# Two stick-breaking heads scored together on halves of TensorE's rows, and an earlier split of the first key weights

## The chip, the cores and the metric

The kernel runs on one core of one Trainium2 chip. The time is the device time of one execution in microseconds (us). Times before and after are medians of several executions of the same inputs; the profile is of one more execution.

## The reference, cut to what matters

Two transformer blocks over 512 positions of width 1024 are computed, one after the other. Only the first block matters here. Its input x is normed, scaled and shifted by a modulation that is itself computed from c (`mod = c @ w_ada + b_ada`), and projected by one wide matrix:

```python
h = rmsnorm(x, norm_gain) * (1.0 + scale) + shift
proj = h @ w_in
(sb_q, sb_k, sb_v, sb_z, c_q, c_kv, k_rot, mla_z, g_a, g_b) = split(proj)
# stick-breaking attention, 8 heads of 64, for each block of 128 queries
z = einsum('bhqd,bhkd->bhqk', qb, k) * scale
log_one_minus = where(strict, log_sigmoid(-z), 0.0)
suffix = cumsum(log_one_minus, reverse=True) - log_one_minus
w = where(strict, exp(log_sigmoid(z) + suffix), 0.0)
out = einsum('bhqk,bhkd->bhqd', w, v)
```

The second block has, among other things, a forgetting attention ("fox", also 8 heads of 64) and a per-layer embedding (PLE) whose small projection `p @ w_ple_proj` needs nothing of x; the kernel computes that projection first of all. Inputs and outputs are float32.

## The kernel before, in words

**Engines.** Each engine runs one written-out program (`tensor_program`, `scalar_program`, `vector_program`, `pool_program`, `sync_program`) in its own order. They meet at semaphores. A name such as `SBQK` or `HI` is a semaphore with the count that each key stands for. An engine never passes over a wait: what stands behind it stands still.

**Split weights and activations.** A projection is computed from a high part (float32 rounded to the fp32r format) and a low part (the rest) of weights and activations. One output tile of 128 x 512 with contraction 1024 is 8 x 3 = 24 matmuls of 128 x 512 (`project`, line 673; every matmul is recorded at line 650 in `mm`). The names are `whi`, `wlo` for the weights, `hhi`, `hlo` for the activations h, and `phi`, `plo` for the PLE inputs.

**Weights in chunks.** `chunks()` (line 34) lists the weights in the order of use. A chunk of 128 x 1024 is loaded by SyncE into one of 3 buffers `raw`; ScalarE copies its high part to one of 4 buffers `whi` (line 1341); VectorE subtracts, which gives `wlo` (line 1824). Both engines do that in `conv(name, idx)`, which splits all chunks up to two behind the named one in the list (`LOOK = 2`). A buffer of the four can be written again once the projection of four chunks earlier is done. In the list, the eight chunks that follow the stick-breaking values (cq 0 to 2, ckv 0 and 1, kr, sz 0 and 1) each have a chunk `ada` of the modulation behind them, which VectorE multiplies and sums directly from `raw` (line 1835, into `mod`). In that part of the list, two chunks ahead are one `ada` and one weight chunk only; behind it, two chunks ahead are two weight chunks.

**The first stage.** TensorE does the PLE projection (chunks `pp`), then the stick-breaking queries (`sbq`, four chunks) block by block of h as the modulation comes (`project_group`). ScalarE evicts each block of the turned x twice (`modulated`, line 1380): to `tmpf` in full float32 and to `hhi` rounded; VectorE subtracts for `hlo`. After it TensorE projects `sbk` 0 to 3 and the values `sbv`.

**The stick-breaking stage.** `sb_qk(h)` computes the scores of one head (keys x queries, 512 + 384 + 256 + 128 columns) in three banks of PSUM, with contraction over 128 rows. Two heads share a tile of keys `kp`, so the queries `qp` of each head have a tile of their own of which the other head's 64 rows are zero (written by GpSimd at line 579). Then, for head h: VectorE takes the minimum with 40 (`sb_pre`, line 1988), ScalarE does exp and log(1 + x) (lines 1465 and 1467), VectorE takes a maximum (`sb_pre2`), ScalarE writes the high part `sph`, GpSimd (896 of the columns, line 567) and VectorE (256) write the low part `spl`; TensorE adds the suffix sums (`sb_suffix`), ScalarE does exp (`sb_weights`, line 1480), and `sb_pv` multiplies two heads by the values. `sph` and `spl` are one buffer each, so head h + 1 may write them only after the suffix of head h.

**The fillers.** Between these steps TensorE does 21 further steps of projections, the fillers (`filler_a`, one `yield` for each): cq 0 to 2, ckv 0 and 1, kr, sz 0 to 3, mz 0 to 3, ga 0 to 5, and ga 6 and 7 together. All but one of the first 20 write to bank 7. ScalarE and VectorE run the same generator in their own programs: VectorE copies the filler's bank out and calls `conv` for the coming chunks, ScalarE calls `conv`. Of the fillers named here by number, F0 is cq 0, F5 is kr, F6 is sz 0, F13 is mz 3, F14 is ga 0, F19 is ga 5. The order on TensorE before, for each pair of heads, is: scores of h + 1, filler, suffix of h, filler, scores of h + 2, filler, suffix of h + 1, filler, values of the pair, filler.

The fox stage of the second block has the form that the change brings to the first: `fox_qk` (line 1021) computes the scores of two heads in turn, each with contraction over 64 rows, and then the masks of both.

Of the kernel before, what the change touches and what calls it, by code (L numbers as in the profile page):

```python
# [169 lines left out]
def build(nc, w_all, cst_d, rc_d, gc_d, rm_d, vec_d, x_d, xn_d, c_d, pos_d, ada_d, p_d, out_d):  # L170
# [7 lines left out]
    WN = {i: w for w, i in enumerate(WCH)}  # L178

# [6 lines left out]
    with top:  # L186
# [54 lines left out]
        with ExitStack() as s1:  # L241
            qp = sb(s1, "qp", [128, 8, S])
            kp = sb(s1, "kp", [128, 4, S])
            sbv = sb(s1, "sbv", [128, 4, S])
            sp = sb(s1, "sp", [128, 2, 1280])
            sph = sb(s1, "sph", [128, 1280], F32R)
            spl = sb(s1, "spl", [128, 1280], F32R)
# [116 lines left out]
        def weights_of(name, idx):  # L364
            i = PIDX[name, idx]
            _, _, kb, n = PLAN[i]
            w = WN[i]
            hi, lo = (x[:, w % NHL, 0:kb * n].rearrange("p (k n) -> p k n", k=kb) for x in (whi, wlo))
            return hi, lo, w

# [18 lines left out]
        def turn_bank(h, kb):  # L389
# [45 lines left out]
        QZERO = sig("pool_qzero", (0, 1))  # L435
        QPE, KPE, SBV = sig("act_qp", range(8)), sig("dve_kp", range(4)), sig("act_sbv", range(4))
        SBQK, SBMIN, SBLN, SBMAX, SBHI, SBLO0, SBLO1, SBSUF = (
            sig(n, range(8)) for n in ("pe_sbqk", "dve_sbmin", "act_sbln", "dve_sbmax", "act_sbhi", "pool_sblo",
                                       "dve_sblo", "pe_sbsuf"))
# [109 lines left out]
        def pool_program(e):  # L549
# [10 lines left out]
            def sb_low(h):  # L560
                G.wait_ge(*QZERO(1))
                G.wait_ge(*SBHI(h))
                if h > 1:
                    G.wait_ge(*ROPED("kr"))
                if h:
                    G.wait_ge(*SBSUF(h - 1))
                e.tensor_tensor(spl[:, 0:896], sp[:, h % 2, 0:896], fr(sph[:, 0:896]), ALU.subtract).then_inc(SBLO0.sem, 1)  # L567

# [5 lines left out]

            G.wait_ge(*proj("pp", 1, 3))
            for r in range(2):
                if r:
                    G.wait_ge(*QZERO(0))
                e.memset(qp[64 - 64 * r:128 - 64 * r, :, :].rearrange("p (m r) n -> p m r n", r=2)[:, :, r, :], 0.0
                         ).then_inc(QZERO.sem, 1)  # L580

# [24 lines left out]
            for h in range(8):  # L606
                sb_low(h)
                if h == 1:
                    rope_sum("kr", krs[64:96, :], 0)
# [35 lines left out]
        def tensor_program(e):  # L645
# [32 lines left out]
            def project_group(chs, act, order=range(8), split=True, between=None):  # L678
# [4 lines left out]
                def high(name, idx, m, b, k):  # L683
                    hi, lo, w = weights_of(name, idx)
                    if split:
                        T.wait_ge(*HI(key(k)))
# [83 lines left out]
            for m in range(4):  # L770
                free[m] = [QPE(2 * m + 1)]
# [7 lines left out]
            def filler_a():  # L779
                for m in range(5):  # L780
                    project(*(("cq", m) if m < 3 else ("ckv", m - 3)), 128, 7, h1)
                    free[7] = [CQ(m)]
# [9 lines left out]
                T.wait_ge(*SS(("c", 4)))  # L792
                sum_squares(6, "kv", ssq[:, :])
                for m in range(8):
                    project(*(("sz", m) if m < 4 else ("mz", m - 4)), 128, 7, h1)
                    free[7] = [ZE(m)]
                    yield
                for m in range(6):
                    b = 0 if m == 4 else 7
# [8 lines left out]
            def sb_qk(h):  # L808
                T.wait_ge(*QPE(h))
                T.wait_ge(*QZERO(h % 2))  # L810
                T.wait_ge(*KPE(h // 2))
                T.wait_ge(*CONST())
                for kb in KB_ORDER:
                    out = sb_out(h, kb)
                    bank(3 * (h % 2) + BK[kb])
                    mm(out, kp[:, h // 2, 128 * kb:128 * kb + 128], qp[:, h, 128 * kb:512], kb != 3, False)
                    t = mm(out[:, 0:128], identB, msB, False, False)
                t.then_inc(SBQK.sem, 1)

            def sb_suffix(h):  # L820
# [5 lines left out]
                T.wait_ge(*SBLO0(h))  # L826
                T.wait_ge(*SBLO1(h))
# [23 lines left out]
            sb_qk(0)  # L851
            next(fa)
            for pr in range(4):
                h = 2 * pr
                sb_qk(h + 1)
                next(fa)
                sb_suffix(h)
                next(fa)
                if pr < 3:
                    sb_qk(h + 2)  # L860
# [4 lines left out]
                if pr < 3:  # L865
                    next(fa)
# [469 lines left out]
        def scalar_program(e):  # L1336
# [6 lines left out]
            def conv(name, idx=0, look=LOOK):  # L1343

                while split_to[0] < min(PIDX[name, idx] + 1 + look, len(PLAN)):
# [6 lines left out]
                    if w >= NHL:  # L1352
                        A.wait_ge(*used(w - NHL))
                    copy(whi[:, w % NHL, 0:n], raw[:, i % NRAW, 0:n]).then_inc(WHI.sem, 1)
# [19 lines left out]
            def modulated(b):  # L1374
# [4 lines left out]
                for out in (tmpf[:, b % 2, :], hhi[:, b, :]):  # L1379
                    t = e.activation(out, PB[4 + b % 4][:, :], ACT.Identity, scale=mod[:, 8 + b:9 + b], bias=mod[:, b:b + 1])  # L1380
                t.then_inc(HI.sem, 1)
# [22 lines left out]
            for b in range(NB):  # L1404
                modulated(b)
                if b == 0:
                    conv("sbq", 3, 0)

            conv("sbq", 3)
            for m in range(4):  # L1410
                A.wait_ge(*proj("sbq", m))
                for r in range(2):
                    copy(qp[64 * r:64 * r + 64, 2 * m + r, :], PB[m][64 * r:64 * r + 64, :], scale=0.125
                         ).then_inc(QPE.sem, 1)
# [17 lines left out]
            def filler_a():  # L1432
# [14 lines left out]
                A.wait_ge(*CQN(2))  # L1447
                root(rsb[:, :], 6, 256, "kv")
                for m in range(8):
                    conv(*(("sz", m) if m < 4 else ("mz", m - 4)))  # L1450
# [1192 lines left out]
```

## Time and profile before

| what | value |
|---|---|
| median of 3 executions | 1234.1 us (1234.05 to 1234.74) |
| profiled execution, its time | 1235.34 us |
| its span | 1233.5 us |
| TensorE busy | 97% of the span |
[...]
| chain of work that ended last, share of TensorE | 85% |

The span is from the first to the last instruction in the profile; the execution's own time is 1.8 us longer. A record of a matmul shows its start and a modelled end, and following matmuls overlap, so the time that one takes is read from start to start. "Idle before" in brackets is counted from the modelled end of the record before, which is later than the start at which the next could have followed.

### The profile page before, as it was taken

How to read it: one execution, taken by the hardware profiler on the slowest of the kernel's cores; microseconds unless marked ns; L12 is line 12 of the kernel's file. 1: busy time of each engine (PE TensorE's matmuls, PEld its weight loads, DVE VectorE, ACT ScalarE, POOL GpSimd, SP SyncE). 2: the span in 40 equal slices, each digit the busy share in tenths (PEclk: the TensorE clock that was granted, in tenths of full speed). 3: DMA queues.
4: the chain of work that ended last, by engine and by line, in shares of the span. 5: the costliest groups of instructions: out<-in, count | busy, mean ns of one | idle time of the engine just before them, and what ended most of it. 6: DMA issues, size and time to landing. Idle time of an engine off the chain costs nothing.

```text
span 1233.5 us, 15994 instructions
## 1 busy us (share of the span) xinstructions
PE 1199.7 (97%) x6548; PEld 964.2 (78%) x6548; DVE 701.2 (57%) x1086; ACT 500.9 (41%) x799; POOL 92.3 (7%) x72
## 2 busy tenths in 40 slices
PE   7999999999999999999999999999999999999996
PEld 5787777777777787887777788878888888888885
DVE  6644564359556676457887785364444444433356
ACT  5424434454454455224446545253233223322244
POOL 0390010104000000000000200000000000000000
PEclk9999999999999999999999999999999999999998
DMA  9732322213121343331112101123322222433322
GB/s 370 282 109 71 125 92 84 69 59 101 52 69 52 97 142 98 105 120 45 59 54 84 34 4 36 52 86 103 103 89 100 99 89 98 144 99 100 104 86 71
DMA packets 35593, 118.22 MB, mean 96 GB/s; under 512 B 3936, under 2 KB 6112, under 8 KB 35520
## 3 DMA queue, kind: packets, MB, share of 16 engines
q1 hardware_dynamic: 33024, 111.03, 26.9%
q0 software_dynamic: 1392, 4.72, 1.3%
q10 hardware_dynamic: 1104, 1.45, 0.3%
q8 instruction: 52, 0.85, 0.3%
q14 instruction: 21, 0.17, 0.0%
HBM read 112.99 MB, written 4.19 MB: 95 GB/s over the span
## 4 chain that ended last, share of the span: by engine, by line
PE 85%; DVE 6%; ACT 5%; issue 2%; POOL 0%; DVEq 0%; ACTq 0%
PE pb L650 82%; PE pb L906 1%; DVE wlo L1824 1%; PE pb L736 1%; ACT mP L1539 1%; DVE mnm L2066 1%; DVE xT L1824 1%; ACT whi L1341 1%; ACT Y L1341 1%; DVE mP L2056 1%; DVE junk L1835 0%; PE pb L1068 0%; ACT xT L1560 0%; DVE sp L1824 0%; ACT fv L1341 0%
## 5 line engine op out<-in xcount | busy, mean ns | idle before, releaser
L650 PE MATMUL pb<-hlo,whi 128*128 128x512 f32 (+2 forms) x1056 | 408.9, 394 | 7.1 <-DVE wlo L1824 5.9
L650 PE MATMUL pb<-hhi,wlo 128*128 128x512 f32 (+2 forms) x1056 | 410.8, 389 | 2.6 <-DVE wlo L1824 2.6
L650 PE MATMUL pb<-hhi,whi 128*128 128x512 f32 (+2 forms) x1056 | 409.9, 388 | 0.0
L1824 DVE TENSOR_TENSOR wlo<-raw,whi 128x1024 fp32r<-128x1024 f32 (+1 forms) x178 | 216.1, 1219 | 109.0 <-ACT whi L1341 108.0
L650 PEld LDWEIGHTS pb<-hlo,whi 128*128 128x128 f32 (+1 forms) x1056 | 198.5, 188 | 55.2 <-DVE wlo L1824 8.6
L650 PEld LDWEIGHTS pb<-hhi,wlo 128*128 128x128 f32 (+1 forms) x1056 | 198.1, 188 | 44.0 <-DVE wlo L1824 3.5
L650 PEld LDWEIGHTS pb<-hhi,whi 128*128 128x128 f32 (+1 forms) x1056 | 198.1, 188 | 41.0
L1341 ACT ACTIVATE whi<-raw 128x1024 fp32r<-128x1024 f32 (+1 forms) x178 | 181.5, 1034 | 72.9 <-PE pb L650 67.9
L650 PE MATMUL pb<-alo,whi 128*128 128x512 f32 x176 | 68.5, 389 | 0.0
L650 PE MATMUL pb<-ahi,wlo 128*128 128x512 f32 x176 | 68.5, 389 | 0.0
L650 PE MATMUL pb<-ahi,whi 128*128 128x512 f32 x176 | 68.5, 389 | 0.0
L1341 ACT ACTIVATE ahi<-tmpf 128x512 fp32r<-128x512 f32 x22 | 13.9, 632 | 100.5 <-DVE tmpf L1824 100.5
L1341 ACT ACTIVATE hhi<-xT,vec 128x512 fp32r<-128x512 f32 x16 | 11.6, 724 | 84.4 <-DVE xT L1824 84.4
L1824 DVE TENSOR_TENSOR xT<-xT,pb 128x512 f32<-128x512 f32 x16 | 10.9, 684 | 57.1 <-PE pb L650 57.1
L1824 DVE TENSOR_TENSOR tmpf<-pb,rsb 128x512 f32<-128x512 f32 (+1 forms) x31 | 20.9, 674 | 35.8 <-PE pb L650 29.5
L1762 ACT ACTIVATE tmpf<-tmpf 128x512 f32<-128x512 f32 x22 | 13.9, 632 | 64.3 <-DVE tmpf L1824 64.3
L650 PEld LDWEIGHTS pb<-alo,whi 128*128 128x128 f32 x176 | 33.0, 188 | 6.9
L650 PEld LDWEIGHTS pb<-ahi,wlo 128*128 128x128 f32 x176 | 33.0, 188 | 6.9
L650 PEld LDWEIGHTS pb<-ahi,whi 128*128 128x128 f32 x176 | 33.0, 188 | 6.8
L1824 DVE TENSOR_TENSOR sq<-pb,rsb 128x512 f32<-128x512 f32 x22 | 15.2, 692 | 39.4 <-PE pb L650 39.4
L1539 ACT ACTIVATE mP<-pb,mnm 128x512 f32<-128x512 f32 (+3 forms) x32 | 16.4, 526 | 33.4 <-DVE mnm L2046 33.4
L567 POOL TENSOR_TENSOR spl<-sp,sph 128x896 fp32r<-128x896 f32 x8 | 18.8, 2347 | 127.4 <-ACT sph L1341 127.4
(363 smaller groups left out, 1632.6 us busy)
## 6 DMA issues: line engine op xcount, KB each, us to landing
raw<-w_all SPq DMA_DIRECT2D x173, 512.0 KB, 3.5
adab<-ada_d SPq DMA_DIRECT2D x12, 512.0 KB, 12.5
raw<-w_all SPq DMA_DIRECT2D x10, 384.0 KB, 3.0
xT<-xn_d SPq DMA_DIRECT2D x4, 512.0 KB, 12.9
gbt<-ada_d SPq DMA_DIRECT2D x4, 512.0 KB, 15.7
ple_scratch<-zs SPq DMA_DIRECT2D x8, 256.0 KB, 12.2
xT<-x_d POOLq DMA_DIRECT2D x8, 256.0 KB, 3.2
out_d<-xT SPq DMA_DIRECT2D x6, 256.0 KB, 2.6
```

What stands on the lines that cost most here:

```text
L567: e.tensor_tensor(spl[:, 0:896], sp[:, h % 2, 0:896], fr(sph[:, 0:896]), ALU.subtract).then_inc(SBLO0.sem, 1)
L650: return e.matmul(out, lhs, rhs, start=start, stop=stop, skip_group_check=True)
L736: t = e.matmul(PB[b][:, :], ones, src, start=True, stop=more is None)
L906: t = e.transpose(PB[b][:, o + 128 * (qi - kb):o + 128 * (qi - kb) + 128], P[:, PO[qi] + 128 * kb:PO[qi] + 128 * kb + 128], ident)
L1341: return e.activation(out, in_, ACT.Copy, **kw)
L1539: t = e.activation(d, src, ACT.Exp, bias=nm[:, i, qi:qi + 1], accum_out=rs[:, i, qi:qi + 1])
L1762: e.activation(tmpf[:, j % 2, :], tmpf[:, j % 2, :], ACT.Silu).then_inc(SG.sem, 1)
L1824: return e.tensor_tensor(out, a, b, op)
L2056: t = e.tensor_scalar(d, d, rs[:, i, qi:qi + 1], None, ALU.mult)
L2066: t = e.tensor_reduce(mnm[:, h % 2, qi:qi + 1], src, AX.X, ALU.max)
```

## The change

**Scores on halves of the rows.** `qp` becomes four tiles, one for each pair of heads, without zeros; ScalarE copies each projected tile in one instruction instead of two, and GpSimd's two fills of zeros go. `sb_qk(pr)` computes both heads of a pair, head r with contraction over the 64 rows from 64 r, alternating between the heads, then all the masks. It needs all six banks 0 to 5 at once.

**A new order of the stage.** For each pair: scores of both heads, three fillers in a row, suffix of h, a filler, suffix of h + 1, a filler, values. Fillers with number 1, 6, 11 and 16 write to bank 6. The sum of squares for ckv moves from ahead of sz 0 to ahead of sz 2. ScalarE's order is: exp and log of h, exp and log of h + 1, high part of h, (in the last pair the Silu of sz, with its two table loads), three fillers, high part of h + 1, exp of h, filler, exp of h + 1, filler. VectorE's order is: minimum of h, minimum of h + 1, maximum of h, filler, maximum of h + 1, low part of h, two fillers, low part of h + 1, two fillers. The low part is VectorE's alone; GpSimd does none of it.

**The first keys' weights.** The chunk sbk 0 is split into `phi` and `plo`, which are free once the PLE projection is done. ScalarE does it between the blocks 6 and 7 of h, VectorE ahead of the low part of block 7. The chunks behind it move up one buffer in the ring of four. `qp` moves behind `kp` and `sbv` in memory.

**The modulated blocks.** ScalarE writes `hhi` first, with a semaphore of its own (`HI1`) for which TensorE waits, and `tmpf` second.

```diff
+        def split_at(w, n):
+            if w == WK0:
+                return phi[:, :, :].rearrange("p a b -> p (a b)"), plo[:, :, :].rearrange("p a b -> p (a b)")
+            r = (w if w < WK0 else w - 1) % NHL
+            return whi[:, r, 0:n], wlo[:, r, 0:n]
+        def filler_bank(i):
+            return 6 if i % 5 == 1 else 7
+        def room(w):
+            if w == WK0:
+                return [proj("pp", 1, 3)]
+            at = w - NHL if w < WK0 or w - NHL > WK0 else w - NHL - 1
+            return [used(at)] if at >= 0 else []
...
+            def sb_qk(pr):
+                T.wait_ge(*QPE(pr))
+                T.wait_ge(*KPE(pr))
+                T.wait_ge(*CONST())
                 for kb in KB_ORDER:
-                    out = sb_out(h, kb)
-                    bank(3 * (h % 2) + BK[kb])
-                    mm(out, kp[:, h // 2, 128 * kb:128 * kb + 128], qp[:, h, 128 * kb:512], kb != 3, False)
-                    t = mm(out[:, 0:128], identB, msB, False, False)
-                t.then_inc(SBQK.sem, 1)
+                    for r in range(2):
+                        bank(3 * r + BK[kb])
+                        rows = slice(64 * r, 64 * r + 64)
+                        mm(sb_out(r, kb), kp[rows, pr, 128 * kb:128 * kb + 128], qp[rows, pr, 128 * kb:512], kb != 3, False)
+                for r in range(2):
+                    for kb in KB_ORDER:
+                        t = mm(sb_out(r, kb)[:, 0:128], identB, msB, False, False)
+                    t.then_inc(SBQK.sem, 1)
...
             for pr in range(4):
                 h = 2 * pr
-                sb_qk(h + 1)
-                next(fa)
+                sb_qk(pr)
+                for _ in range(3):
+                    next(fa)
                 sb_suffix(h)
-                next(fa)
-                if pr < 3:
-                    sb_qk(h + 2)
                 next(fa)
                 sb_suffix(h + 1)
                 next(fa)
                 sb_pv(pr)
-                if pr < 3:
-                    next(fa)
...
+                for out, sem_ in ((hhi[:, b, :], HI1.sem), (tmpf[:, b % 2, :], HI.sem)):
+                    e.activation(out, PB[4 + b % 4][:, :], ACT.Identity, scale=mod[:, 8 + b:9 + b], bias=mod[:, b:b + 1]
+                                 ).then_inc(sem_, 1)
...
                 modulated(b)
                 if b == 0:
                     conv("sbq", 3, 0)
+                if b == 6:
+                    conv("sbk", 0, 0)
...
-                for r in range(2):
-                    copy(qp[64 * r:64 * r + 64, 2 * m + r, :], PB[m][64 * r:64 * r + 64, :], scale=0.125
-                         ).then_inc(QPE.sem, 1)
+                copy(qp[:, m, :], PB[m][:, :], scale=0.125).then_inc(QPE.sem, 1)
...
             for pr in range(4):
                 h = 2 * pr
+                sb_pre(h)
+                sb_pre(h + 1)
+                sb_high(h)
                 if pr == 3:
                     e.preload_act_table_set(SILU)
...
+                for _ in range(3):
+                    next(fa)
+                sb_high(h + 1)
                 sb_weights(h)
...
+            def sb_low(h):
                 V.wait_ge(*SBHI(h))
                 if h:
                     V.wait_ge(*SBSUF(h - 1))
-                tt(spl[:, 1024:], sp[:, h % 2, 1024:], fr(sph[:, 1024:]), ALU.subtract).then_inc(SBLO1.sem, 1)
+                for o, n in ((0, 896), (1024, 256)):
+                    t = tt(spl[:, o:o + n], sp[:, h % 2, o:o + n], fr(sph[:, o:o + n]), ALU.subtract)
+                t.then_inc(SBLO.sem, 1)
...
             for pr in range(4):
                 h = 2 * pr
+                sb_pre(h)
+                if pr == 0:
+                    conv("cq", 0)
+                sb_pre(h + 1)
+                sb_max(h)
                 next(fa)
-                sb_pre(h + 1)
+                sb_max(h + 1)
+                sb_low(h)
                 next(fa)
-                sb_pre2(h + 1)
+                next(fa)
+                sb_low(h + 1)
                 next(fa)
                 next(fa)
                 V.wait_ge(*SBPV(pr))
-                e.tensor_copy(qp[:, h, :], PB[6][:, :]).then_inc(OA.sem, 1)
+                e.tensor_copy(qp[:, pr, :], PB[6][:, :]).then_inc(OA.sem, 1)
```

## Rows read from the trace of the kernel before

**Rows 1.** The page: span and busy time of each engine.

```profile
span 1233.5 us, 15994 instructions
...
PE 1199.7 (97%) x6548; PEld 964.2 (78%) x6548; DVE 701.2 (57%) x1086; ACT 500.9 (41%) x799; POOL 92.3 (7%) x72
```

**Rows 2.** Timeline of TensorE (start us, us), the first pair of heads.

```profile
101.19 1.02 PE L650 MATMUL pb<-qp,kp 128*128 128x512 f32 x2
...
103.71 0.48 PE L650 MATMUL pb<-hlo,whi 128*128 128x512 f32 x1
...
112.43 0.47 PE L650 MATMUL pb<-hlo,whi 128*128 128x512 f32 x1 [0.48 <-DVE gbt L1951]
...
118.00 1.05 PE L650 MATMUL pb<-sp,cst 128*128 128x128 f32 x8
...
121.28 0.50 PE L650 MATMUL pb<-hlo,whi 128*128 128x512 f32 x1 [0.33 <-DVE wlo L1824]
```

**Rows 3.** Timeline of TensorE: a suffix and what follows it; the stage's end.

```profile
135.72 1.05 PE L650 MATMUL pb<-sp,cst 128*128 128x128 f32 x8
...
138.51 1.02 PE L736 MATMUL pb<-ssq,cst 128*128 128x512 f32 x2
...
271.96 0.50 PE L650 MATMUL pb<-hlo,whi 128*128 128x512 f32 x1
```

**Rows 4.** Timeline of TensorE in the fox stage: values, scores, next projection.

```profile
581.80 2.37 PE L650 MATMUL pb<-fPT,fv 128*64 128x512 f32 x16
584.10 2.43 PE L650 MATMUL pb<-fk,fqo 64*128 64x512 f32 x16
...
586.89 0.48 PE L650 MATMUL pb<-hlo,whi 128*128 128x512 f32 x1
```

**Rows 5.** Timeline around the end of the query projection, ScalarE, VectorE, TensorE.

```profile
50.62 0.78 ACT L1380 ACTIVATE tmpf<-pb,mod 128x512 f32<-128x512 f32 x1 [2.08 <-issue]
...
52.10 0.69 DVE L1824 TENSOR_TENSOR hlo<-tmpf,hhi 128x512 fp32r<-128x512 f32 x1 [1.56 <-ACT hhi L1380]
...
57.54 0.50 PE L650 MATMUL pb<-hlo,whi 128*128 128x512 f32 x1 [1.79 <-DVE wlo L1824]
```

**Rows 6.** Timeline of VectorE, after F1, and after F6 of before.

```profile
120.00 1.22 DVE L1824 TENSOR_TENSOR wlo<-raw,whi 128x1024 fp32r<-128x1024 f32 x1
...
163.42 1.41 DVE L1827 SCALAR_TENSOR_TENSOR gbt<-gbt,vec,rsb 128x512 f32<-128x512 f32 x2
```

**Rows 7.** Timeline of ScalarE: exp and log of head 2, then the Silu.

```profile
150.57 1.28 ACT L1465 ACTIVATE sp<-sp 128x1280 f32<-128x1280 f32 x1 [4.11 <-DVE sp L1988]
...
153.15 1.04 ACT L1341 ACTIVATE whi<-raw 128x1024 fp32r<-128x1024 f32 x1
...
159.22 1.28 ACT L1341 ACTIVATE sph<-sp 128x1280 fp32r<-128x1280 f32 x1 [5.03 <-DVE sp L1824]
...
244.31 1.28 ACT L1491 ACT_TABLE_LOAD   x1
...
247.81 1.28 ACT L1495 ACT_TABLE_LOAD   x1
```

**Rows 8.** Timeline of VectorE at head 2: minimum, then a split that waits.

```profile
148.93 1.61 DVE L1988 TENSOR_SCALAR sp<-pb 128x512 f32<-128x512 f32 x3
...
154.23 1.23 DVE L1824 TENSOR_TENSOR wlo<-raw,whi 128x1024 fp32r<-128x1024 f32 x1 [2.49 <-ACT whi L1341]
```

**Rows 9.** Windows of 1 us: length, TensorE busy (instructions), granted clock, DMA.

```profile
29.00:30.00 1.00, 0.00 (x0) 0.77 1.04 414
...
32.00:33.00 1.00, 1.00 (x5) 0.52 1.02 410
...
166.00:167.00 1.00, 0.00 (x0) 1.00 0.00 0
...
1223.00:1224.00 1.00, 0.00 (x0) 1.00 0.00 0
1224.00:1225.00 1.00, 0.95 (x2) 0.61 0.00 0
```

More of the change, by code:

```diff
@@ L178, in build @@
     WN = {i: w for w, i in enumerate(WCH)}
+    WK0 = WN[PIDX["sbk", 0]]
     def pieces(name, i):
@@ L367, in weights_of @@
             w = WN[i]
-            hi, lo = (x[:, w % NHL, 0:kb * n].rearrange("p (k n) -> p k n", k=kb) for x in (whi, wlo))
+            hi, lo = (x.rearrange("p (k n) -> p k n", k=kb) for x in split_at(w, kb * n))
             return hi, lo, w
+        def split_at(w, n):
[3 more added lines that the diff above has]
+            return whi[:, r, 0:n], wlo[:, r, 0:n]
         def sb_out(h, kb):
@@ L433, in build @@
         ZPLE = sig("act_zple", range(8))
[L435 to L439, printed above, removed]
+        HI1 = sig("act_hi1", range(NB))
+        QPE, KPE, SBV = sig("act_qp", range(4)), sig("dve_kp", range(4)), sig("act_sbv", range(4))
+        SBQK, SBMIN, SBLN, SBMAX, SBHI, SBLO, SBSUF = (
+            sig(n, range(8)) for n in ("pe_sbqk", "dve_sbmin", "act_sbln", "dve_sbmax", "act_sbhi", "dve_sblo", "pe_sbsuf"))
         SBW = sig("act_sbw", [(h, b) for h in range(8) for b in range(3)])
@@ L605, in pool_program @@
             e.tensor_scalar(ang[:, :], ang[:, :], lim, -lim, ALU.min, ALU.max).then_inc(ANG.sem, 1)
[L606 to L609, printed above, removed]
+            rope_sum("kr", krs[64:96, :], 0)
             G.wait_ge(*ZA(3))
@@ L770, in tensor_program @@
             for m in range(4):
-                free[m] = [QPE(2 * m + 1)]
+                free[m] = [QPE(m)]
             for m in range(4):
@@ L780, in filler_a @@
                 for m in range(5):
-                    project(*(("cq", m) if m < 3 else ("ckv", m - 3)), 128, 7, h1)
-                    free[7] = [CQ(m)]
+                    b = filler_bank(m)
+                    project(*(("cq", m) if m < 3 else ("ckv", m - 3)), 128, b, h1)
+                    free[b] = [CQ(m)]
                     if m == 3:
@@ L791, in filler_a @@
                 yield
-                T.wait_ge(*SS(("c", 4)))
-                sum_squares(6, "kv", ssq[:, :])
                 for m in range(8):
-                    project(*(("sz", m) if m < 4 else ("mz", m - 4)), 128, 7, h1)
-                    free[7] = [ZE(m)]
+                    b = filler_bank(6 + m)
+                    if m == 2:
+                        T.wait_ge(*SS(("c", 4)))
+                        sum_squares(6, "kv", ssq[:, :])
+                    project(*(("sz", m) if m < 4 else ("mz", m - 4)), 128, b, h1)
+                    free[b] = [ZE(m)]
                     yield
                 for m in range(6):
-                    b = 0 if m == 4 else 7
+                    b = filler_bank(14 + m)
                     project("ga", m, 128, b, h1)
@@ L864, in tensor_program @@
                 sb_pv(pr)
-                if pr < 3:
-                    next(fa)
             next(fa)
@@ L1351, in conv @@
                     A.wait_ge(*RAW(i))
-                    if w >= NHL:
-                        A.wait_ge(*used(w - NHL))
-                    copy(whi[:, w % NHL, 0:n], raw[:, i % NRAW, 0:n]).then_inc(WHI.sem, 1)
+                    for s, v in room(w):
+                        A.wait_ge(s, v)
+                    copy(split_at(w, n)[0], raw[:, i % NRAW, 0:n]).then_inc(WHI.sem, 1)
             def root(dst, b, n, key, bias=eps_c, scale=0.0):
@@ L1483, in scalar_program @@
             conv("cq", 0)
-            sb_pre(0)
-            sb_pre2(0)
-            next(fa)
             for pr in range(4):
                 h = 2 * pr
-                next(fa)
+                sb_pre(h)
+                sb_pre(h + 1)
+                sb_high(h)
                 if pr == 3:
@@ L1502, in scalar_program @@
                 next(fa)
-                if pr < 3:
-                    sb_pre(h + 2)
-                    next(fa)
-                    sb_pre2(h + 2)
             next(fa)
@@ L1854, in conv @@
                     V.wait_ge(*WHI(w))
-                    tt(wlo[:, w % NHL, 0:n], raw[:, i % NRAW, 0:n], fr(whi[:, w % NHL, 0:n]), ALU.subtract
-                       ).then_inc(WLO.sem, 1)
+                    hi, lo = split_at(w, n)
+                    tt(lo, raw[:, i % NRAW, 0:n], fr(hi), ALU.subtract).then_inc(WLO.sem, 1)
             def low(key, out, src, hi):
@@ L1905, in vector_program @@
                     low(("1", k), hlo[:, k, :], tmpf[:, k % 2, :], hhi[:, k, :])
+            conv("sbk", 0, 0)
             low(("1", 7), hlo[:, 7, :], tmpf[:, 1, :], hhi[:, 7, :])
@@ L1975, in filler_a @@
                     V.wait_ge(*proj("ga", m))
-                    e.tensor_copy(gax[:, m, :], PB[0 if m == 4 else 7][:, :]).then_inc(GAE.sem, 1)
+                    e.tensor_copy(gax[:, m, :], PB[filler_bank(14 + m)][:, :]).then_inc(GAE.sem, 1)
                     conv("ga", m)
@@ L2015, in vector_program @@
                 V.wait_ge(*SBPV(pr))
-                e.tensor_copy(qp[:, h, :], PB[6][:, :]).then_inc(OA.sem, 1)
-                if pr < 3:
-                    sb_pre(h + 2)
-                    next(fa)
-                    sb_pre2(h + 2)
+                e.tensor_copy(qp[:, pr, :], PB[6][:, :]).then_inc(OA.sem, 1)
             for m in range(4):
```

58 lines of the change are left out of this document (14 added, 44 removed).

## The prediction

> **What bounds the kernel.** I read the page first. TensorE is busy for 1199.7 of 1233.5 us [rows 1], so whatever moves the time must either take work off TensorE or change how long it stands still. The profiled execution took 1235.34 us, 1.8 us more than its span and 1.2 us more than the median of 1234.1. All sums below are changes of the span; I add them to the median. I then followed TensorE's timeline through the stage that the change rewrites, and looked at each start that has idle time in brackets. The stage begins with the first scores at 101.19 [rows 2] and ends where filler 20 (ga 6) starts, at 271.96 [rows 3]: 170.8 us.
>
> The unit prices, from start to start: scores of one head 103.71 − 101.19 = 2.5 us; one filler that follows something else 118.00 − 112.43 = 5.57, taken as 5.55; a suffix 138.51 − 135.72 = 2.79 [rows 2, 3]. A pair's values cost 584.10 − 581.80 = 2.3 us, by the fox stage, where they have the same form [rows 4]. A sum of squares takes 0.9. The stage of before is then 8 × 2.54 + 20 × 5.55 + 8 × 2.79 + 4 × 2.3 + 2 × 0.86 = 164.5 us of work (2.54, a head's mean, is the 2.52 plus start-up), and TensorE stands still for the other 6.3 us. Such a stop is seen ahead of 112.43 and of 121.28 [rows 2].
>
> **Scores of two heads: less work.** Before, a pair costs 2 × 2.54 = 5.1 us. The trace has the new form already: in the fox stage both heads, with their masks and each on 64 rows, take 586.89 − 584.10 = 2.79 us [rows 4]. The other three pairs of that stage, which aren't shown, take 2.79 each as well. So each pair saves 2.3 us, four save 9.2. The bounds are 0 (the halves do not overlap here) and this 9.2; I take 9.2, since shapes and order are the same. The four fillers that now directly follow a filler save 0.1 each, the start-up, 0.4 in all.
>
> [...]
>
> **The first pair waits for a bank.** The pair needs banks 0 to 5, and banks 3 to 5 hold the values `sbv`, which ScalarE only then copies out. Before, head 1 came 5.5 us later. The wait is one eviction, 0.6 us, and its start-up, at least 0 if the other half runs on beside it and at most 1.0: I take 0.7.
>
> **Three fillers in a row: new stops.** This is the main term. Up to sz 1, `conv` after a filler splits one `ada` chunk and only the next filler's weights. From the end of F1 to the earliest start of F2 VectorE has to copy the bank out, multiply the `ada` chunk, and split: 121.28 − 118.00 = 3.28 us [rows 2]; the split itself starts at 120.00 and frees TensorE 1.28 us later [rows 6]. Before, the suffix (2.79) lay in this gap and 0.5 remained. After the change nothing lies between F1 and F2, nor between F6 and F7:
>
> - F1 to F2 (cq 2): 3.28 us. The same pace for F6 to F7 (sz 1): 3.28.
> - F2 to F3, where the suffix lies between: 3.28 − 2.79 = 0.5. F3 to F4 and F7 to F8 have a suffix and a sum of squares between them (3.65), so nothing. F8 to F9 (sz 3) has no `ada` chunk, but the two products of ckv (1.41 us [rows 6]) instead, so again about 3.3 − 2.8 = 0.5.
> - F5 to F6 (sz 0). Here ScalarE is late. Its copy of sz 0's high part stands behind exp and log of both heads and the high part of the first. Before, VectorE already waited 2.49 us for it behind one head [rows 8]. Counted from the pair's start: scores 2.8; minimum, until exp starts, 150.57 − 148.93 = 1.64 [rows 7, 8]; exp and log of two heads 2 × (153.15 − 150.57) = 5.16; the high part 1.2 (1.28, which overlaps the next by 0.1); the weights' copy, until VectorE starts, 154.23 − 153.15 = 1.08; the split until TensorE starts 1.28 [rows 6 to 8]. That is 13.1 us. F5 ends at 2.79 + 5.55 = 8.3. The stop is 4.8 us.
> - F16 to F17 (ga 3), last pair. The same chain, with the Silu and its two table loads ahead of the fillers: 247.81 + 1.28 − 244.31 = 4.8 more [rows 7], so 17.9 us. Before, this block lay in a longer wait of ScalarE. F16 ends at 2.79 + 5.55 + 5.45 = 13.8. The stop is 4.1 us.
> - F11 to F12 (mz 2): the chain is ready at 13.1, F11 ends at 13.8. No stop, with 0.7 to spare; two weight chunks are split ahead from here on.
>
> Sum of the stops: 0.7 + 3.28 + 0.5 + 4.8 + 3.28 + 0.5 + 4.1 = 17.2 us against 6.3 before, 10.9 more. With −9.2 − 0.4 the stage is 1.3 us longer at the same clock. The stages behind it keep their order.
>
> **The rest of VectorE's and GpSimd's work.** VectorE takes over 896 columns of the low part, about 1.0 us for each head (estimated from 1.2 us for 1024 columns [rows 6]), and GpSimd's wait for it (before, up to 0.8 us once) goes. The low part of the first head falls between two fillers' ends, that of the second under a filler of 5.55, in which high part and low part together take 2.8. Both are free. Without that cover each would cost 1.4. GpSimd's fills of zeros stood ahead of the angles, which are late next for nobody on TensorE. DMA queues carry the same chunks in the same order.
>
> **The first keys' weights.** TensorE stands still from about 55.6 to 57.54, 1.9 us in starts, since sbk 0 is split only when a buffer is free [rows 5]. Now ScalarE copies it (1.0 us) in the 2.08 us in which it waits ahead of block 7, and VectorE splits it (1.2) in the 1.56 us in which it waits ahead of the low part at 52.10 [rows 5]. Both fit, so block 7 isn't later. Its weights are loaded long before. This saves 1.9; the bound from below is 0. With this gap gone, sbk 1 is needed at 61 and split by 57.5.
>
> **High part first.** It lets TensorE start a block 0.7 us earlier. But in this stage TensorE waits for weights early, and later reaches each block 0.8 us or more after it is written. The low part still needs both. I cost it at nothing; the bounds are 0 and −0.7.
>
> **The clock.** Sum so far: +1.3 − 1.9 = −0.6 us. But stops of 3 us and more don't occur in this stage before. TensorE's granted clock fell at 29.54, after 3 us in which it had stood still for most of the time, and came back at 32.96: 0.77 in the first of these windows, 0.52 in the last [rows 9]. [...] At the end it fell at 1224.2, after a stop of 1.9 us; after the 1.7 us ahead of 167.23 it did not [rows 9]. The four long stops of the new order (3.3, 4.8, 3.3, 4.1) are all longer than either. Each can cost between 0 and 1.7. I take three falls of 1.45, 4.3 us, and all of it delays what follows, since the next stop is counted from the filler's end. [...]
>
> The forecast: 1234.1 − 0.6 + 4.3 = 1237.8, say 1238.0.
>
> **The rivals.**
> 1. The clock holds, or falls once. Then 1233.5 to 1235.0, the same as before. For it: it held through 1.7 and 1.8 us. It decides the sign if fewer than two stops bring a fall.
> 2. ScalarE's and VectorE's splits are in time for F6 and F17 (one mechanism: the weights' copy isn't behind exp and log). Then 8.9 us of stops and two falls go: 1238.0 − 8.9 − 2.9 = 1226.2. It decides from 3 us less. For it: `raw` is there early; against it: the order is written out in the program.
> 3. The halves don't overlap, 1238.0 + 9.2 = 1247. Against it: rows 4.
>
> **Chances.** Forecast 0.55, rival 1 0.25, rival 2 0.15, rival 3 0.03, unnamed, slower 0.02. A difference of 0.2%, 2.5 us, is about what a measurement of this kernel can tell. Faster 0.15, within 0.2% 0.26, slower 0.59. The range goes from below rival 1, with half of the split's uncertainty (−2), to all four falls at 1.7 (+2.5) and 1 us for the first wait: 1231.5 to 1241.5. It leaves out rivals 2 and 3.
>
> **What would show it.** TensorE's timeline should have stops of about 3.3 us ahead of cq 2 and sz 1, 4.8 ahead of sz 0, and 4.1 ahead of ga 3, all put down to the split on VectorE; a pair's scores at 2.8 us; no stop ahead of sbk 0, whose projection starts at 55.6; granted clock near 0.5 for some windows behind the long stops. The forecast is wrong if the clock stays at 1.00 there, or if the stops are shorter than the chains say.

## The result and the profile after

The changed kernel takes 1241.93 us (median of 9, 1238.03 to 1243.77), the kernel before beside it 1235.15 (median of 9): 6.8 us more by the medians. The ratio over all executions is 1.0045, interval 1.0032 to 1.0058, which is 5.6 us. A second set of 10 executions gave 1.0031 (1.0019 to 1.0043). The forecast was 1238.0, 3.9 us (0.3%) above the 1234.1 from which it started, in a range of 1231.5 to 1241.5. The kernel before took 1 us more beside this run than that 1234.1, so the comparison goes by the ratio: 1234.1 × 1.0045 = 1239.7, inside the range. The median 1241.93 taken by itself lies 0.4 above it.

The profiled execution took 1239.99 us, its span is 1238.2. TensorE is busy for less time and the span is longer (page of the kernel after, first the span, then busy us by engine):

```profile
span 1238.2 us, 15968 instructions
...
PE 1194.1 (96%) x6548; PEld 961.7 (78%) x6548; DVE 707.6 (57%) x1094; ACT 497.5 (40%) x795; POOL 66.1 (5%) x62
```

TensorE's timeline of the kernel after, the starts that answer to [rows 2 to 5]; in brackets the idle time ahead and what ended it:

```profile
54.22 0.39 PE L649 MATMUL pb<-hlo,phi 128*128 128x512 f32 x1
...
97.83 3.18 PE L649 MATMUL pb<-qp,kp 64*128 64x512 f32 x16
...
101.37 0.48 PE L649 MATMUL pb<-hlo,whi 128*128 128x512 f32 x1
...
115.66 0.50 PE L649 MATMUL pb<-hlo,whi 128*128 128x512 f32 x1 [3.12 <-DVE wlo L1817]
...
126.11 0.50 PE L649 MATMUL pb<-hlo,whi 128*128 128x512 f32 x1 [0.33 <-DVE wlo L1817]
...
143.19 2.43 PE L649 MATMUL pb<-qp,kp 64*128 64x512 f32 x16
...
145.98 0.45 PE L649 MATMUL pb<-hlo,whi 128*96 128x512 f32 x1
...
156.28 0.80 PE L649 MATMUL pb<-hlo,whi 128*128 128x512 f32 x1 [4.52 <-DVE wlo L1817]
...
167.35 0.50 PE L649 MATMUL pb<-hlo,whi 128*128 128x512 f32 x1 [3.12 <-DVE wlo L1817]
...
187.07 0.50 PE L649 MATMUL pb<-hlo,whi 128*128 128x512 f32 x1 [0.45 <-DVE wlo L1817]
...
233.17 2.43 PE L649 MATMUL pb<-qp,kp 64*128 64x512 f32 x16
...
251.20 0.80 PE L649 MATMUL pb<-hlo,whi 128*128 128x512 f32 x1 [4.07 <-DVE wlo L1817]
...
278.21 0.50 PE L649 MATMUL pb<-hlo,whi 128*128 128x512 f32 x1
```

The reader is to see four long stops, ahead of cq 2 (115.66), sz 0 (156.28), sz 1 (167.35) and ga 3 (251.20), where the kernel before had none longer than 1.8 us in this part. Ahead of sbk 0 (54.22), where before stood 1.8 us, there is none. A pair of heads takes 145.98 − 143.19 = 2.79 us.

One more thing is read in the record of a matmul itself. At 156.28 and 251.20 it lasts 0.80 us instead of 0.50: the clock had fallen already in the stop (granted clock 0.50 from 154.5 and from 250.0 on). The windows from each stop's end to the next step (length, TensorE busy, granted clock, DMA share, GB/s) show how far:

```profile
115.66:122.83 7.17, 7.17 (x25) 0.76 0.39 143
156.28:164.25 7.97, 7.95 (x24) 0.70 0.19 66
167.35:174.53 7.18, 7.17 (x24) 0.76 0.40 139
251.20:259.30 8.10, 8.10 (x25) 0.67 0.39 129
```

Each of these is one filler of 24 matmuls, which takes 5.6 us at a granted clock of 1.00 (windows of "TensorE kept busy in the stops", below). Here they take 7.2, 8.0, 7.2 and 8.1.

**The balance.** The scores begin at 97.83 instead of 101.19, 3.4 us earlier. The fall of the clock at 29.5 [rows 9] did not happen in this execution (granted clock 1.00 from 29 to 33), but that explains only a small part. The kernel of the experiment "VectorE's splits before the wait alone", below, has the first stage of before, and its profile has no fall there either (1.00 from 28 to 33). Its timeline of TensorE:

```profile
51.94 0.50 PE L650 MATMUL pb<-hhi,wlo 128*128 128x512 f32 x1 [0.43 <-ACT hhi L1380]
...
57.17 0.50 PE L650 MATMUL pb<-hlo,whi 128*128 128x512 f32 x1 [2.20 <-DVE wlo L1824]
...
100.83 1.02 PE L650 MATMUL pb<-qp,kp 128*128 128x512 f32 x2
```

Without the fall TensorE comes to block 7 before ScalarE has written it, and then stands longer ahead of sbk 0 than the 1.79 us of [rows 5]. So between these two executions of the old first stage the fall cost 0.4 us, not 1.45, and the change's edits to this stage are worth 100.83 − 97.83 = 3.0 us where the clock holds. Each figure is from one execution.

The stage takes 278.21 − 97.83 = 180.4 us instead of 170.8, 9.6 more. Behind it 960.0 us follow instead of 961.5; the profile of before had a fall of the clock at 708.8 us (granted clock 0.50 from 709 to 712) that this one has not (1.00 from 706 to 713). −3.4 + 9.6 − 1.5 = 4.7, the difference of the spans.

ScalarE's timeline of the kernel after shows why sz 0 and ga 3 come late, beside [rows 7]. The weights' copy `whi` stands behind two heads' exp and log, and in the last pair behind the Silu too:

```profile
147.63 1.27 ACT L1464 ACTIVATE sp<-sp 128x1280 f32<-128x1280 f32 x1 [5.23 <-DVE sp L1982]
148.94 1.36 ACT L1466 ACTIVATE sp<-sp,epsc 128x1280 f32<-128x1280 f32 x1
150.21 1.25 ACT L1464 ACTIVATE sp<-sp 128x1280 f32<-128x1280 f32 x1
151.50 1.36 ACT L1466 ACTIVATE sp<-sp,epsc 128x1280 f32<-128x1280 f32 x1
152.77 1.25 ACT L1339 ACTIVATE sph<-sp 128x1280 fp32r<-128x1280 f32 x1
153.93 1.04 ACT L1339 ACTIVATE whi<-raw 128x1024 fp32r<-128x1024 f32 x1
...
244.04 1.28 ACT L1488 ACT_TABLE_LOAD   x1
245.33 2.19 ACT L1491 ACTIVATE zs<-zs 128x512 f32<-128x512 f32 x4
247.54 1.28 ACT L1492 ACT_TABLE_LOAD   x1
248.84 2.95 ACT L1339 ACTIVATE whi<-raw 128x1024 fp32r<-128x1024 f32 x3
```

### The profile page after: what moved, and what is told of

Read it like the earlier page. It is cut to its first block, busy times and chain, and to the rows that moved or that the text cites. A ratio compares the mean times of both kernels' runs of the same rounds, so it can differ in the third digit from the quotient of the medians.

```text
span 1238.2 us, 15968 instructions
## 1 busy us (share of the span) xinstructions
PE 1194.1 (96%) x6548; PEld 961.7 (78%) x6548; DVE 707.6 (57%) x1094; ACT 497.5 (40%) x795; POOL 66.1 (5%) x62
## 3 DMA queue, kind: packets, MB, share of 16 engines
q10 hardware_dynamic: 1104, 1.45, 0.3%
## 4 chain that ended last, share of the span: by engine, by line
PE 85%; DVE 6%; ACT 5%; issue 2%; DVEq 0%; ACTq 0%
PE pb L649 82%; PE pb L904 1%; DVE wlo L1817 1%; PE pb L735 1%; ACT mP L1532 1%; DVE mnm L2063 1%; DVE xT L1817 1%; ACT whi L1339 1%; ACT Y L1339 1%; DVE mP L2053 1%; ACT sp L1464 0%; ACT sp L1466 0%; PE pb L1066 0%; ACT xT L1553 0%; DVE tmpf L1817 0%
## 5 line engine op out<-in xcount | busy, mean ns | idle before, releaser
L1817 DVE TENSOR_TENSOR wlo<-raw,whi 128x1024 fp32r<-128x1024 f32 (+2 forms) x177 | 213.9, 1213 | 113.9 <-ACT whi L1339 113.0
L1339 ACT ACTIVATE whi<-raw 128x1024 fp32r<-128x1024 f32 (+2 forms) x177 | 180.5, 1035 | 91.4 <-PE pb L649 67.4
L1817 DVE TENSOR_TENSOR tmpf<-pb,rsb 128x512 f32<-128x512 f32 (+1 forms) x31 | 20.9, 674 | 35.8 <-PE pb L649 29.5
L1820 DVE SCALAR_TENSOR_TENSOR gq<-cbuf,vec,gq 128x512 f32<-128x512 f32 x36 | 27.1, 752 | 1.3
```

The source lines that it names most:

```text
L1339: return e.activation(out, in_, ACT.Copy, **kw)
L1817: return e.tensor_tensor(out, a, b, op)
L1820: return e.scalar_tensor_tensor(out, a, s, b, op0, op1)
```

## The experiments

The first four ran side by side; medians are given in us with the ratio to before in that set (1235.99; later sets 1235.96 and 1236.03). Differences between two variants are differences of medians.

**The changed kernel again.**

> The changed kernel once more, as the yardstick for the runs beside it. Theory (the stops in the order of fillers, and the clock that falls in them): 1.0045 of before, some 5 us more, with the four stops of 3.1, 4.5, 3.1 and 4.1 us at the same places, and low granted clock behind three or four of them. Rival (the extra time is the chip's drift from run to run): a ratio within 0.998 to 1.002.

1240.38, ratio 1.0031 (1.0019 to 1.0043). In its profile (span 1235.8) the stops are 3.12, 4.52, 3.12 and 4.06 us at the same places, and the clock fell behind three of the four: not ahead of cq 2, where the granted clock was 1.00 from 115.66 to 122 and the filler took 5.6 us. So the stops are fixed by the program, the falls are not. The executions of the changed kernel spread over 4 to 6 us, but those of the kernel before spread as widely (1233.46 to 1239.19 in this set), so the spread is no effect of the change. In both sets the interval lies above 1: the drift rival is out.

**TensorE kept busy in the stops.** The needless matmuls write to the bank that the filler overwrites.

```diff
+            def keep_warm(b, n):
+                bank(b)
+                for _ in range(n):
+                    mm(PB[b][:, :], bcst[:, 0, :], bcst[:, :, :].rearrange("p a b -> p (a b)"), True, True)
...
                     b = filler_bank(m)
+                    if m == 2:
+                        keep_warm(b, 12)
```

> The changed kernel with 12, 18, 12 and 16 needless bf16 matmuls of 128x512 in the four long stops, ahead of the wait for the split weights, into the bank that the filler then overwrites. TensorE is thus busy in the stops, but no stop is shorter. Theory (the clock): the granted clock stays at 1.00 in the stage, the fillers behind the stops take 5.5 us instead of 7.2 to 8.1, and the time falls by 6 to 8.5 us against the changed kernel, to about 0.5 us below before (1.000). Rival (the length of the fillers behind the stops comes from something else, say from VectorE or from the order of banks): no change, 1.0045. If the needless matmuls are themselves too long, the stops grow by up to 1 us each.

1233.98, ratio 0.9983 (0.9972 to 0.9993): 6.4 us less than the changed kernel, and below before. TensorE's timeline of this kernel at the first of the stops, cq 2, and the windows of all four fillers behind them:

```profile
114.24 2.76 PE L649 MATMUL pb<-bcst 128*128 128x512 bf16 x12
...
117.52 0.50 PE L649 MATMUL pb<-hlo,whi 128*128 128x512 f32 x1 [0.52 <-DVE wlo L1828]
```

```profile
117.52:123.12 5.60, 5.60 (x24) 1.00 0.51 187
156.60:162.20 5.60, 5.60 (x24) 1.00 0.28 97
165.48:171.05 5.57, 5.57 (x24) 1.00 0.50 186
247.77:253.35 5.58, 5.58 (x24) 1.00 0.30 98
```

From the end of F1 (114.24) to F2 it is still 3.28 us. Only the clock differs, 1.00 against 0.76, 0.70, 0.76 and 0.67. The four fillers are 1.6 + 2.4 + 1.6 + 2.5 = 8.1 us shorter than in the profile of the changed kernel. The mean granted clock over all executions says the same: 0.988 for the changed kernel in both sets, 0.995 here, 0.994 for the kernel before. That the clock's falls cost this time is shown. The stage, from the first scores to ga 6, takes 272.26 − 99.69 = 172.6 us here, against 180.4.

**Next weights split before the wait.**

```diff
                     n = ("cq", m) if m < 3 else ("ckv", m - 3)
+                    conv(*n)
                     V.wait_ge(*proj(*n))
                     e.tensor_copy(gbt[:, m, :], PB[filler_bank(m)][:, :]).then_inc(CQ.sem, 1)
-                    conv(*n)
```

The same in the loops over sz, mz and ga.

> The changed kernel, but VectorE splits the next filler's weights before it waits for the filler's end, not after it copied the bank out. Theory: the two stops that are VectorE's own pace, ahead of cq 2 and sz 1 (3.1 us each), and the short ones of 0.3 to 0.5 go; those ahead of sz 0 and ga 3 stay, for there ScalarE is late. With two falls of the clock (1.7 us each) that is 6.6 + 3.4 + 0.8, about 10 us less than the changed kernel, 0.9955 to 0.998 of before. Rival (what stops these two fillers is the bank or the load of raw weights): less than 2 us.

1232.35, ratio 0.9964 (0.9951 to 0.9976): 8.0 us less, not 10. The stop ahead of sz 1 is gone. Ahead of cq 2 1.21 us remain: VectorE is busy with maximum and low part of the first heads until then. Ahead of ga 3 the stop is 4.76 us instead of 4.06, now ended by the copy of bank 7: VectorE stands at the split, waits 7.97 us for ScalarE, and the bank's eviction is queued behind (VectorE's timeline, then TensorE's):

```profile
241.93 1.23 DVE L1817 TENSOR_TENSOR wlo<-raw,whi 128x1024 fp32r<-128x1024 f32 x1 [7.97 <-ACT whi L1339]
243.08 0.68 DVE L1971 COPY xT<-pb 128x512 f32<-128x512 f32 x1
...
243.91 0.77 PE L649 MATMUL pb<-hlo,whi 128*128 128x512 f32 x1 [4.76 <-DVE xT L1971]
```

**And the first split of a pair ahead of its exp and log.**

```diff
                 h = 2 * pr
+                if pr:
+                    conv(*(("kr",), ("mz", 0), ("ga", 1))[pr - 1])
                 sb_pre(h)
```

On ScalarE and VectorE, on top of the edit above.

> As the kernel that splits before the wait, and both ScalarE and VectorE split the weights of each pair's second filler's successor before they begin with the pair's scores (kr's, mz 0's and ga 1's place in the list), so ahead of exp, log and the Silu. Theory: all four long stops go, and with them the clock's falls: the stage then is nearly its work, 155 to 157 us against 180.4, so 23 to 25 us below the changed kernel, and 17 to 19 us below before: ratio 0.984 to 0.988. Rival (TensorE then waits for the loads of raw weights, three buffers, or for the softer edges of exp and log): stops of 2 us and more in their place, ratio above 0.990.

1222.47, ratio 0.9884 (0.9864 to 0.9905): 17.9 us less than the changed kernel and 13.5 less than before. The expectation was 23 to 25 less. The stops ahead of sz 0 and ga 3 are gone as the theory said, but sz 1 is not in time. TensorE's timeline of this kernel:

```profile
115.03 0.50 PE L649 MATMUL pb<-hlo,whi 128*128 128x512 f32 x1 [1.21 <-DVE wlo L1819]
...
157.03 0.50 PE L649 MATMUL pb<-hlo,whi 128*128 128x512 f32 x1 [2.60 <-DVE wlo L1819]
```

VectorE's timeline of the same profile, that of `e3_split_early`, ahead of the second stop:

```profile
151.68 1.62 DVE L1819 TENSOR_TENSOR sp<-pb,sp 128x512 f32<-128x512 f32 x3
153.22 1.42 DVE L1819 TENSOR_TENSOR spl<-sp,sph 128x896 fp32r<-128x896 f32 x2
154.55 1.28 DVE L1830 CUSTOM_DVE_ANT_0 junk<-raw,cbt,mod 128x1024 bf16<-128x1024 f32 x1
155.75 0.08 DVE L1830 DVE_READ_ACCUMULATOR2_ANT mod<- 128x1 f32 x1
155.75 1.22 DVE L1819 TENSOR_TENSOR wlo<-raw,whi 128x1024 fp32r<-128x1024 f32 x1
```

VectorE does the maximum and low part of the heads (`sp` and `spl`, from 151.68 to 154.6), which the suffix needs only at 162.61, 5.6 us after the stop's end, before the `ada` chunk (1.28 us) and the split (1.22 us) that TensorE waits for.

The stage takes 258.72 − 99.11 = 159.6 us instead of the expected 155 to 157; these two stops are most of that. The other 2.9 us by which the saving of the stage (180.4 − 159.6 = 20.8) exceeds that of the span (17.9) are falls of the clock elsewhere, in the first stage (granted clock 0.50 from 30 to 33) and at 732.7 (0.50 to 0.51 until 736), that this profile has and that of the changed kernel has not. Behind the stop ahead of sz 1 the clock held here (1.00 from 157.03 to 162.61). In the profiles of three kernels below (sbk 0 in the ring, scores in turn, full part first) it fell there, behind stops of 2.62, 2.21 and 2.57 us, to a mean of 0.70, 0.70 and 0.71 over the next 5.6 to 5.8 us: none of these stops lasted 3 us.

**Two more splits moved.**

```diff
-            conv("cq", 0)
+            conv("cq", 1)
...
                 next(fa)
+                if pr == 1:
+                    conv("sz", 0)
                 sb_max(h + 1)
```

> The kernel with the early splits, and two more splits moved: cq 2's weights ahead of the first pair's exp and log, sz 1's on VectorE ahead of the second head's maximum in the second pair. Theory: the two stops that are left in the stage, 1.2 us ahead of cq 2 and 2.6 us ahead of sz 1, go: 3.5 to 4 us less than the kernel with the early splits, ratio 0.985 to 0.986. Rival (the later maximum and low part now stop the suffix): less than 1 us gained.

1218.88, ratio 0.9863 (0.9849 to 0.9876): 3.6 us less than the one before it. In the stage only one stop is left, and it takes 255.53 − 99.25 = 156.3 us (TensorE's timeline):

```profile
153.85 0.50 PE L649 MATMUL pb<-hlo,whi 128*128 128x512 f32 x1 [0.79 <-DVE wlo L1819]
```

**The parts by themselves, in the kernel with early splits (1222.47).** sbk 0 split in the ring as before (`WK0 = -1`, and the two `conv("sbk", 0, 0)` taken out):

> The kernel with the early splits, but sbk 0 is split into the ring of four buffers as before, after the query projection. Theory: the stop of 1.9 us (1.8 in idle time) ahead of sbk 0 is back, and nothing else: 1.9 us more than the kernel with the early splits, ratio 0.990 against 0.9884. Rival (the stop is then hidden, or the ring's shift matters elsewhere): within 0.5 us of it, or more than 3 us above it.

1226.66, ratio 0.9921 (0.9907 to 0.9936): 4.2 us more. The stop in its profile is 1.78 us. Its first scores begin at 100.12, in an execution without the fall in the first stage (granted clock 1.00 from 29 to 33), and at 97.83 in the profile of the changed kernel, which has none either: 2.3 us. The other 1.9 of the 4.2 are not shown; the intervals allow them to be noise.

The score matmuls in turn:

```diff
-                for kb in KB_ORDER:
-                    for r in range(2):
+                for r in range(2):
+                    for kb in KB_ORDER:
```

> The kernel with the early splits, but the score matmuls of a pair run head after head (all four of rows 0 to 63, then all four of rows 64 to 127), not in alternation. Theory (the saving is two halves of the rows working at once): a pair takes 2 x 2.3 + 0.4 = 5.0 us instead of 2.8, four pairs 8 to 9 us more than the kernel with the early splits, ratio 0.995 to 0.996. Rival (a matmul on 64 rows is by itself half as long): no change.

1227.88, ratio 0.9939 (0.9924 to 0.9955): 5.4 us more. Expected were 8 to 9. A pair takes 145.79 − 141.39 = 4.40 us, not 5.0 (TensorE's timeline of this kernel):

```profile
141.39 4.04 PE L649 MATMUL pb<-qp,kp 64*128 64x512 f32 x16
145.36 0.62 PE L649 MATMUL pb<-bcst 128*128 128x128 bf16 x8
145.79 0.45 PE L649 MATMUL pb<-hlo,whi 128*96 128x512 f32 x1
```

So the alternation is worth 4.40 − 2.79 = 1.6 us for each pair, 6.4 for four. The other 2 × 2.52 − 4.40 = 0.6 come with the rest of the new form: the shorter contraction, and the masks behind all scores, not one behind each. These two were not tried apart. A matmul on 64 rows was not by itself half as long here: a head's scores and masks take 2.20 us in turn on 64 rows and 2.52 on full rows.

The modulated blocks full part first:

> The kernel with the early splits, but each modulated block is written full part first, and TensorE waits for both, as before. Theory: a block is ready 0.7 us later for TensorE; now that TensorE reached block 7 0.2 us before it was written, this could cost up to 0.5 to 0.7 us when the clock didn't fall earlier in the stage, and nothing when it fell (TensorE is then 1.5 us later). So 0 to 0.7 us more. Rival (the order carries a part of the gain): 1.5 us and more.

1222.64, ratio 0.9893 (0.9877 to 0.9908): 0.2 us more, no difference that four executions could tell. Both profiles, this one and that of the kernel with early splits, have the fall in the first stage (granted clock 0.50 from 31 to 33). Whether the order is worth something where the clock holds, as the 0.43 us ahead of block 7 suggest, stays open.

**The parts by themselves, in the kernel before.** The first keys' weights alone, with `split_at` and `room` of the change, and `qp` behind `sbv`:

> The kernel before, with only the first keys' weights split into the PLE buffers (and the queries behind keys and values in memory). Theory: the stop of 1.8 us ahead of sbk 0 goes and nothing else changes: 1.9 us less, ratio 0.9985; up to 1.5 us more if the clock fell in or after that stop in some executions. Rival (the time comes back at a later wait, since VectorE and ScalarE are not earlier): ratio 1.000.

1232.15, ratio 0.997 (0.9956 to 0.9983): 3.9 us less, about 2 more than expected (the interval allows 2.1 to 5.4). Its profile, which has the fall in the first stage as before's (granted clock 0.50 from 31 to 33), begins the scores at 99.44 instead of 101.19, 1.75 us earlier. The stage takes 170.8 us in both. The span is shorter by 1.4 us more because the fall at 708.8 didn't happen (1.00 from 706 to 712). The mean granted clock over its ten executions is 0.9949 against 0.9938 before, worth at most 0.0011 × 1234 = 1.4 us (an estimate). So chance falls elsewhere may hold a good part of the rest, and executions without the fall in the first stage, where the gain is larger, the remainder. That is argued and not shown.

VectorE's splits before the wait alone, in the loops of before:

> The kernel before, with only VectorE's order in the fillers changed: the next weights are split before it waits for the filler's end. Theory: the short stops of the stage that are VectorE's pace (0.33, 0.57, 0.55, 1.66, 0.58 and 0.7 us in idle time) go, 3.5 to 4.5 us less, ratio 0.9964 to 0.9972. Rival (in this order the later copy of the bank, or GpSimd's low part, takes their place): ratio above 0.999.

1231.31, ratio 0.9956 (0.9941 to 0.9971): 4.7 us less. Of the five short stops that the profile of before puts down to VectorE's split (0.33, 0.57, 0.55, 1.66 and 0.58 us), none is left. Two stops that a bank's copy ends remain, 0.48 and 0.26 us, and GpSimd's, 0.27 instead of 0.82. The stage takes 266.93 − 100.83 = 166.1 us instead of 170.8.

This bears on what the scores on halves are worth. If these two gains in the kernel before add up, it would take 1236.0 − 3.9 − 4.7 = 1227.4 us, and the kernel with all moved splits (1218.88) is 8.5 us below that. This is an estimate: the two were not run together.

**The stops of the first stage kept busy.** On top of the kernel with all moved splits:

```diff
                     if k == order[0]:
-                        T.wait_ge(*WLO(w))
                         bank(b)
+                        if name == "sbq" and idx > 1:
+                            for _ in range((4, 6)[idx - 2]):
+                                mm(PB[b][:, :], bcst[:, 0, :], bcst[:, :, :].rearrange("p a b -> p (a b)"), True, True)
+                        T.wait_ge(*WLO(w))
```

> The kernel with all four moved splits, and 4 and 6 needless bf16 matmuls in the two stops of the first stage, ahead of the waits for the weights sbq 2 and sbq 3. Theory (the clock falls behind these stops in most executions and costs 1.4 to 1.7 us): 1 to 1.7 us less than the kernel with all moved splits, ratio 0.985, and granted clock 1.00 from 29 to 35 us. Rival (the fall there costs nothing, since modulation sets the pace of this stage): no change.

1217.08, ratio 0.9839 (0.9822 to 0.9856): 1.8 us less, the fastest kernel here, 19 us below before. The intervals of the two ratios overlap, so the gain is likely and not certain. The granted clock is 1.00 from 29 to 35 us in its profile. In the kernel without these matmuls it had fallen (windows of 1 us, as above):

```profile
30.00:31.00 1.00, 1.00 (x3) 0.50 1.02 406
31.00:32.00 1.00, 1.00 (x4) 0.50 1.09 438
32.00:33.00 1.00, 1.00 (x5) 0.50 1.00 397
```

One profile doesn't show that the matmuls hold the clock here: it held in this stretch without them too, in both profiles of the changed kernel (1.00 from 29 to 33). The mean granted clock over the executions, 0.996 against 0.995, points the same way as the times.

## Why the prediction was right, and what was mis-sized

- **Scores on halves.** Taken at 2.79 us a pair from [rows 4], measured 2.79. The saving of 9.2 us is there.
- **First pair.** Taken at 2.79 + 0.7, measured 101.37 − 97.83 = 3.54.
- **Stops by VectorE's pace.** Taken at 3.28 from end to start, measured 3.28 (112.38, the end of F1, to 115.66); ahead of sz 1 the idle time is the same, 3.12. The short ones were taken at 0.5 each and stand in the profile as 0.33 and 0.45 of idle time.
- **sz 0.** Taken at 13.1 us behind the pair's start, measured 156.28 − 143.19 = 13.09.
- **ga 3.** Taken at 17.9, measured 251.20 − 233.17 = 18.0.
- **The stage at full clock.** Taken at 170.8 + 1.3 = 172.1; measured 180.4, less the 8.1 us that the four slow fillers lost, is 172.3; with TensorE kept busy it is 172.6.
- **sbk 0 and the modulated blocks.** This term was too small. Projection of sbk 0 starts without a stop, as taken. The 1.9 us and the premise that TensorE reaches each block 0.8 us after it is written were read from a profile with the fall in the first stage. There the split is worth 1.75 us. Where the clock holds, all edits to this stage together are worth 3.0, and the medians gave 3.9 and 4.2 us for the split in the two trials. Order of the blocks by itself: nothing that could be told.
- **The clock.** This is the mis-sized term. I took three falls of 1.45 us, 4.3. No run shows this term; it was my estimate, half of the 2.89 us in which TensorE was busy from 29.54 to 32.96, where the granted clock was 0.50, as the bound of 1.7 is half of those 3.42 us (profile of before). In its place, in the profile of the changed kernel the clock fell at all four stops, which cost 1.6 to 2.5 us each, 8.1 in all; with TensorE kept busy the medians give 6.4. I sized a fall by one at which 0.5 us of the slow stretch still lay in the stop [rows 9], and set its upper bound at 1.7. At sz 0 the filler ran at a granted clock of 0.50 for 4.7 us (156.28 to 161.0) and at ga 3 for 5.4 (251.20 to 256.6), longer than the row that I used, and lost more than that bound. The sign of the result hangs on this term: with TensorE kept busy the ratio is 0.9983, by which 1234.1 becomes 1232.0, a little below what rival 1 says for a clock that holds.

**How much of it was luck.** The mechanism held: each long stop stands where the chains put it, with the length that they gave. The closeness of the total is in part luck. By the medians the clock cost 2.1 us more than taken (6.4 for 4.3), and sbk 0 gave 2.0 more than taken (3.9 for 1.9); the two errors have opposite signs.

Rival 2, splits in time, did not happen by itself, but is what the moved splits produce. Rival 3 is out. The gain of the stage went into new waits: by the unit prices 9.6 us of TensorE's work were saved, while the stage at full clock is 172.3 − 170.8 = 1.5 us longer, so 11.1 us of stops came in, and 8.1 us (by the medians 6.4) of low clock on top.

## What to carry to other kernels

When a schedule takes small steps out from between large ones, count what the helpers did in those steps: here a suffix or a head's scores, 2.5 to 2.8 us, were the cover of VectorE's copy, product and split. Give the helpers their work in the order in which TensorE needs the results: the split of the next weights before the wait for the filler's end, and before exp, log and a table switch (here 2 × 2.6 us and, with the Silu, 4.8). Price a stop with what it does to the clock: here stops of 3.1 us lost 1.6 us more behind them, those of 4.5 and 4.1 us 2.4 and 2.5, and the clock also fell behind some of 2.2 to 2.6 us. And a profile with a chance fall of the clock in it is a poor source for what a stop ahead of the stage costs (the stop ahead of sbk 0 was 1.79 us with the fall and 2.20 without it): look at an execution without it too. Where a stop can't be removed, needless matmuls can be tried: here, written into a bank that is overwritten, they held the granted clock at 1.00 in all four fillers behind the stops.

## What the runs showed of the hardware that was not expected

- After a stop of 4.1 us the granted clock was 0.50 for the first 5.4 us of the filler behind it: the one at 251.20 took 8.10 us instead of 5.58. After stops of 3.1 us the fillers took 7.17 and 7.18 us instead of 5.60 and 5.57. In another execution of the same program the first of these stops, ahead of cq 2, brought no fall (granted clock 1.00, its filler took 5.60 us). Behind stops of 2.2 to 2.6 us ahead of sz 1 the clock fell in three profiles (a mean of 0.70 to 0.71 over the next 5.6 to 5.8 us) and held in a fourth (1.00).
- A fall of the clock did not always cost what the slow work lost: between two executions of the old first stage, one with a fall in which TensorE worked for 2.9 us at a granted clock of 0.50 and one without, the first scores began only 0.36 us apart (101.19 and 100.83), since TensorE had later waits that took up the difference (0.43 and 2.20 us without the fall, 1.79 with it).
- The eight score matmuls of a pair (16 records), four on rows 0 to 63 and four on rows 64 to 127, take 145.55 − 143.19 = 2.36 us in alternation and 145.36 − 141.39 = 3.97 in turn.
- One head's float32 scores on full rows with a bf16 mask behind each cost 2.52 us; on 64 rows, in turn and with the masks behind all, a head costs 4.40 / 2 = 2.20.
